# Four x tiles, chunk 0, four x tiles, chunk 2: another order of loads and engines at the start of a transformer layer

## What is computed

```python
c_act = jax.nn.silu(c)
mod = (c_act @ w_ada[l] + b_ada[l])[:, None, :]        # 1 x 6144, w_ada is 1024 x 6144
sh_m, sc_m, g_m, sh_f, sc_f, g_f = jnp.split(mod, 6, axis=-1)

u = layer_norm(x) * (1 + sc_m) + sh_m
z = u @ w_in[l]
z_pool, z_q, z_k, z_v, z_conv, z_gate = jnp.split(z, IN_SPLITS, axis=-1)
...
x = layer_norm(ALPHA * x + g_m * mix_out, ln_mix_g[l], ln_mix_b[l])
u = layer_norm(x) * (1 + sc_f) + sh_f
h = jnp.square(jax.nn.relu(u @ w_ff1[l] + b_ff1[l]))
ff_out = h @ w_ff2[l] + b_ff2[l]
```

## Time and profile before

| what | value |
|---|---|
| median of 3 runs | 1427.4 us |
| the profiled execution, its own time | 1426.88 us |
| span of the profiled execution | 1425.1 us |
| PE busy | 1393.0 us, 98% of the span |
| DVE, ACT, POOL busy | 68%, 45%, 30% |
| mean granted TensorE clock | 0.993 of full speed |

### The profile page before, as it was taken

One profiled execution on the slowest core, in us unless ns is written; L12 is line 12 of the kernel. 1 busy time (PEld: TensorE's weight loads), 2 busy tenths in 40 slices (PEclk: granted clock), 3 DMA queues, 4 the chain that ended last, 5 costly groups with the idle time before them and its releaser, 6 DMA issues.

```text
span 1425.1 us, 17299 instructions
## 1 busy us (share of the span) xinstructions
PE 1393.0 (98%) x6522; PEld 1148.6 (81%) x6522; DVE 969.4 (68%) x1340; ACT 647.3 (45%) x914; POOL 421.8 (30%) x453
## 2 busy tenths in 40 slices
PE   7799999999999999999999999999999999999996
PEld 3688888888888888888888888888888888888885
DVE  5789677776479946464768797556565646437787
ACT  5522677777542124101616774443345535343251
POOL 1006465555566000000024327333444200001315
PEclk9899999999999999999999999999999999999998
DMA  9775465654565232762622555444445878456361
GB/s 347 266 266 159 148 185 156 188 168 149 161 234 172 89 104 79 245 192 86 200 114 89 183 181 193 142 145 146 156 163 207 297 277 299 162 211 236 118 222 60
DMA packets 159083, 256.42 MB, mean 180 GB/s; under 512 B 11352, under 2 KB 81422, under 8 KB 159000
## 3 DMA queue, kind: packets, MB, share of 16 engines
q1 hardware_dynamic: 144152, 204.97, 43.1%
q0 software_dynamic: 14848, 50.34, 10.5%
HBM read 182.36 MB, written 68.71 MB: 176 GB/s over the span
## 4 chain that ended last, share of the span: by engine, by line
PE 91%; DVE 5%; ACT 2%; issue 1%; DMA 1%; SPq 0%; DVEq 0%; ACTq 0%
PE ps L2065 24%; PE ps L2067 24%; PE ps L2066 24%; PE ps L2214 11%; PE ps L2254 2%; PE ps L2264 2%; PE ps L2279 2%; PE ps L2085 1%; DVE part_lo L1922 1%; PE ps L2129 1%; PE ps L2404 1%; DVE q L1983 0%; DMA k_raw<-tw_scratch 0%; DMA ada<-in_w_ada_dram 0%; DVE w_lo L1387 0%
## 5 line engine op out<-in xcount | busy, mean ns | idle before, releaser
L2065 PE MATMUL ps<-act_hi,w_hi 128*128 128x512 f32 (+1 forms) x480 | 187.2, 390 | 9.4 <-DVE act_lo L1482 9.4
L1922 DVE TENSOR_TENSOR part_lo<-k_raw,part_hi 128x1024 fp32r<-128x1024 f32 x112 | 146.1, 1332 | 58.6 <-ACT part_hi L935 55.4
L2067 PE MATMUL ps<-act_hi,w_lo 128*128 128x512 f32 (+1 forms) x480 | 184.6, 385 | 0.0
L2066 PE MATMUL ps<-act_lo,w_hi 128*128 128x512 f32 (+1 forms) x480 | 184.6, 385 | 0.0
L2065 PE MATMUL ps<-part_hi 128*128 128x512 f32 x448 | 174.3, 389 | 0.0
L2066 PE MATMUL ps<-part_lo,part_hi 128*128 128x512 f32 x448 | 174.3, 389 | 0.0
L2067 PE MATMUL ps<-part_hi,part_lo 128*128 128x512 f32 x448 | 174.3, 389 | 0.0
L935 ACT ACTIVATE part_hi<-k_raw 128x1024 fp32r<-128x1024 f32 x112 | 116.4, 1059 | 113.6 <-DMA k_raw<-tw_scratch 48.8
L2065 PEld LDWEIGHTS ps<-act_hi,w_hi 128*128 128x128 f32 x480 | 91.1, 190 | 28.4 <-issue 5.9
L1387 DVE TENSOR_TENSOR w_lo<-w_raw,w_hi 128x1024 fp32r<-128x1024 f32 x51 | 65.9, 1291 | 65.6 <-ACT w_hi L935 65.6
L2066 PEld LDWEIGHTS ps<-act_lo,w_hi 128*128 128x128 f32 x480 | 91.2, 190 | 18.4 <-issue 1.0
(11 more groups left out here) (260 smaller groups left out, 3202.4 us busy)
## 6 DMA issues: line engine op xcount, KB each, us to landing
k_raw<-h_scratch SPq DMA_DIRECT2D x112, 256.0 KB, 4.2
w_raw<-in_w_in_dram SPq DMA_DIRECT2D x42, 512.0 KB, 4.1
ada<-in_w_ada_dram SPq DMA_DIRECT2D x8, 2048.0 KB, 9.6
tw_rows<-in_w_ff_dram POOLq DMA_DIRECT2D x64, 256.0 KB, 4.1
tw_scratch<-tw_sum POOLq DMA_DIRECT2D x32, 512.0 KB, 3.7
h_scratch<-h_sum POOLq DMA_DIRECT2D x64, 256.0 KB, 3.0
k_raw<-tw_scratch SPq DMA_DIRECT2D x64, 256.0 KB, 5.4
pair_raw<-in_w_ff_dram SPq DMA_DIRECT2D x13, 1024.0 KB, 6.3
```

Of the source, the lines that this page charges most:

```text
L1922: nc.vector.tensor_tensor(part_lo[s][:, :, :], k_raw[rs][:, :, :], f(part_hi[s][:, :, :]), ALU.subtract)\
L2065: nc.tensor.matmul(out, sh, mh, start=first, stop=False)
L2066: nc.tensor.matmul(out, sh, ml, start=False, stop=False)
L2067: return nc.tensor.matmul(out, sl, mh, start=False, stop=last)
```

## The change

The change touches the first 60 us only.

1. **Loads.** SP now issues x tiles 0 to 3, the whole of chunk 0, x tiles 4 to 7, the small rows, the whole of chunk 2, weight blocks 0 and 1, chunk 1, weight block 2, chunk 3. Before, the two halves of chunks 0 and 2 alternated with pairs of x tiles, and chunk 3 stood ahead of weight block 2. Each chunk is still two loads, for chunk 2 now 6 + 2 row blocks (`SPLIT`).
2. **PE.** Four transposed tiles, the row of chunk 0 in one piece, four transposed tiles, the row of chunk 2. PE does only k = 0..5 of chunk 2, DVE k = 6 and 7 (`ada_chunk(2)`); of chunk 3 PE does k = 0..3 (`row_chunk(3, 0)`, placed in the first projection ahead of block 2), DVE k = 4..7. `row_columns(2)` and `row_columns(3)` sum both parts, in eight matmuls instead of four. `row_columns(1)` and `(3)` move up by two k: they stand behind k = 0, 1 of block 2 instead of behind k = 3.
3. **DVE and ACT** go through the x tiles one by one, each step of a tile offset by one: statistics of tile t, then `scale_bias` of tile t-1; on ACT root of t, norm of t-1, copy of t-2. The copies of tiles 6 and 7 are now made by DVE. The copy of the bias columns (`cols`) moves behind them.
4. **`keep_active`**: 24 new transposes of the identity on PE, eight each after `row_columns(2)`, after `mod_done` 1 and after the first `u_tmp`; their output is not used.
5. Semaphore counts follow the new numbering (`N_DIRECT` 2 to 1).

The core of the diff:

```diff
-N_DIRECT = 2
+N_DIRECT = 1
+SPLIT = {0: 4, 1: 4, 2: 6, 3: 4}
...
-ADA_BANKS = {0: 0, 2: 1}
+ADA_BANKS = {0: 0, 2: 1, 3: 6}
...
-                    sp.wait_ge(partial_done, 1)
+                    sp.wait_ge(partial_done, 2)
...
+                    sp.wait_ge(partial_done, 1)
...
-                    sp.wait_ge(partial_done, 2)
+                    sp.wait_ge(head_ps_done, 5)
+                    sp.wait_ge(partial_done, 3)
...
             def load_ada_half(i, half):
-                ks = slice(4 * half, 4 * half + 4)
+                ks = (slice(0, SPLIT[i]), slice(SPLIT[i], 8))[half]
...
-            load_ada_half(0, 0)
-            load_x(range(2))
-            load_ada_half(0, 1)
-            load_x(range(2, 4))
+            load_x(range(4))
+            load_ada(0)
+            load_x(range(4, ST))
...
-            load_ada_half(2, 0)
-            load_x(range(4, 6))
-            load_ada_half(2, 1)
-            load_x(range(6, ST))
+            load_ada(2)
...
+            load_block(1)
...
-            load_block(1)
+            load_block(2)
...
-            load_block(2)
...
             def save_ada_row(i):
-                act.wait_ge(head_ps_done, {0: 1, 2: 4}[i])
+                act.wait_ge(head_ps_done, {0: 1, 2: 4, 3: 5}[i])
...
             def save_tile(i):
...
-            for i in range(0, ST, 2):
+            for i in range(ST):
...
-                take_root(i + 1, i + 1)
-                norm(i, i, mid[:, i, :])
-                if i + 1 < ST - 1:
-                    norm(i + 1, i + 1, mid[:, i + 1, :])
-                if i == 2:
-                    save_ada_row(0)
-                if i == ST - 2:
-                    save_ada_row(2)
-                    cut_hi(0)
-                    save_tile(i)
-                else:
-                    save_tile(i)
-                    save_tile(i + 1)
+                if i >= 1:
+                    norm(i - 1, i - 1, mid[:, i - 1, :])
+                if i >= 2:
+                    save_tile(i - 2)
+            save_ada_row(0)
+            save_ada_row(2)
+            cut_hi(0)
...
+            save_ada_row(3)
...
-            for i in range(0, ST, 2):
-                for t in (i, i + 1):
-                    dve.wait_ge(x_in[t], 16)
-                    stats(mid[:, t, :], t)
-                for t in (i, i + 1):
-                    scale_bias(t, t)
-                if i == 4:
-                    dve.wait_ge(head_ps_done, 3)
-                    nc.vector.tensor_copy(cols[:, 0:ROWS_A], ps[:, 7, PIECE:PIECE + ROWS_A])
-                    nc.vector.tensor_copy(cols[:, ROWS_A:ROWS_A + ROWS_C], ps[:, 7, PIECE + P:PIECE + P + ROWS_C])\
-                        .then_inc(cols_done, 1)
+            for t in range(ST):
+                dve.wait_ge(x_in[t], 16)
+                stats(mid[:, t, :], t)
+                if t >= 1:
+                    scale_bias(t - 1, t - 1)
+            scale_bias(ST - 1, ST - 1)
...
             def start_chunk(i):
...
-                dve.wait_ge(ada_in[i % 3], 16 * (i // 3 + 1))
+                if i == 1:
+                    dve.wait_ge(ada_in[1], 16)
+                elif i in (2, 3):
+                    dve.wait_ge(ada_end_in[i % 3], 16 * (i // 3 + 1))
+                else:
+                    dve.wait_ge(ada_in[i % 3], 16 * (i // 3 + 1))
...
-                link(nc.vector.tensor_scalar(partial_of(i)[:, :], ada[i % 3][:, 0, :], c_act[:, 0:1], None, ALU.mult))
-                add_rows(i, range(1, 4))
+                k0 = SPLIT[i] if i in (2, 3) else 0
+                link(nc.vector.tensor_scalar(partial_of(i)[:, :], ada[i % 3][:, k0, :], c_act[:, k0:k0 + 1], None,
+                                             ALU.mult))
+                add_rows(i, range(k0 + 1, 4))
...
             def end_chunk(i):
-                if i in (1, 3):
-                    dve.wait_ge(ada_end_in[i % 3], 16 * (i // 3 + 1))
-                add_rows(i, range(4, 8))
+                if i == 1:
+                    dve.wait_ge(ada_end_in[1], 16)
+                add_rows(i, range({2: 7, 3: 5}.get(i, 4), 8))
...
+            for t in (ST - 2, ST - 1):
+                dve.wait_ge(z_done, t + 1)
+                dve.wait_ge(x_copied, ST - 2)
+                nc.vector.tensor_copy(x_t[:, :, t * P:(t + 1) * P], tile_banks(t)).then_inc(x_copied, 1)
+            dve.wait_ge(head_ps_done, 3)
+            nc.vector.tensor_copy(cols[:, 0:ROWS_A], ps[:, 7, PIECE:PIECE + ROWS_A])
+            nc.vector.tensor_copy(cols[:, ROWS_A:ROWS_A + ROWS_C], ps[:, 7, PIECE + P:PIECE + P + ROWS_C])\
+                .then_inc(cols_done, 1)
+            ada_chunk(2)
...
-            dve.wait_ge(z_done, ST)
-            nc.vector.tensor_copy(x_t[:, :, (ST - 1) * P:ST * P], tile_banks(ST - 1)).then_inc(x_copied, 1)
...
             def row_chunk(i, half):
...
-                pe.wait_ge((ada_in, ada_end_in)[half][i % 3], 16)
-                for k in range(4 * half, 4 * half + 4):
+                pe.wait_ge((ada_in, ada_end_in)[half][i % 3], 32 if i == 3 else 16)
+                for k in range(4 if half else 0, 8 if half else SPLIT[i]):
...
-                                           start=k == 0, stop=k == 7)
+                                           start=k == 0, stop=k == (7, None, 5, 3)[i])
...
             def row_columns(i):
...
-                if i in (0, 2):
-                    pe.wait_ge(head_sb_done, 3 + i // 2)
-                else:
+                if i != 1:
+                    pe.wait_ge(head_sb_done, {0: 3, 2: 4, 3: 5}[i])
+                if i > 0:
+                    pe.wait_ge(partial_done, {2: 1, 1: 2, 3: 3}[i])
+                if i in (1, 3):
...
-                    pe.wait_ge(partial_done, 1 + i // 2)
...
-                    if i in (0, 2):
-                        ins = nc.tensor.matmul(out, ada_row[i][:, ms], ones_row[0:1, 0:1], start=True, stop=True)
-                    else:
-                        ins = nc.tensor.matmul(out, partial_of(i)[:, ms], ones_row[:, 0:1], start=True, stop=True)
+                    if i != 1:
+                        ins = nc.tensor.matmul(out, ada_row[i][:, ms], ones_row[0:1, 0:1], start=True, stop=i == 0)
+                    if i > 0:
+                        ins = nc.tensor.matmul(out, partial_of(i)[:, ms], ones_row[:, 0:1], start=i == 1, stop=True)
...
+            for i in range(4):
+                transpose_x(i)
...
-            transpose_x(0)
-            transpose_x(1)
...
-            transpose_x(2)
-            transpose_x(3)
+            for i in range(4, 7):
+                transpose_x(i)
+            transpose_x(7)
...
-            row_chunk(2, 0)
-            transpose_x(4)
+            row_chunk(2, 0).then_inc(head_ps_done, 1)
...
-            transpose_x(5)
-            row_chunk(2, 1).then_inc(head_ps_done, 1)
-            transpose_x(6)
...
-            transpose_x(7)
+
+            def keep_active():
+                for m in range(8):
+                    nc.tensor.transpose(ps[:, 0, m % 4 * P:(m % 4 + 1) * P], ident[:, :], ident[:, :])
+
+            keep_active()
+            pe.wait_ge(mod_done, 1)
+            keep_active()
+            pe.wait_ge(u_step, 1)
+            keep_active()
...
+            pe.wait_ge(mod_done, 1)
+            row_chunk(3, 0).then_inc(head_ps_done, 1)
...
-            for k in range(4):
+            for k in range(2):
...
+            for k in range(2, 4):
+                rows_part(2, k)
```

## The result

The changed kernel takes 1437.2 us (median of four runs, 1436.12 to 1439.3) against 1427.9 us (four runs, 1426.52 to 1428.69; a fourth one moved its median up from 1427.4) of the kernel before: a ratio of 1.007, 95% interval 1.0057 to 1.0083. That is 9.4 us slower; forecast were 1436.4 us, 1432.5 to 1440.0.

A forecast was written before the change was run, and what follows sets the result against it. PE was taken as the bound nearly everywhere, so a later start of its dense work moves the end; first knot +8.6 and second +0.4 gave +9.0 us, 1436.4 us, with a range of 1432.5 to 1440.0 for 8 in 10.

The forecast's parts named there:

- First knot: PE's opening of k = 0..3, up to the start of `u_tmp`: 44.4 instead of 35.77 us, costing 8.6 us.
- cold loss: Half clock in tile 3 and the row of chunk 0 after idle PE: 2.0 us taken, from 1.35 to 2.8.
- the pause ahead of tile 6: PE idles 1.5 us because ACT copies tile 4, behind chunk 0's row, before it normalises tile 6.
- Second knot: From `u_tmp` to PE's restart at k = 4: new PE work less the cold restart saved costs 0.4 us.
- `row_columns(1)` 0.9; `row_columns(3)` 1.9: Durations in us forecast for the columns of chunks 1 and 3 on PE, behind k = 0, 1 of block 2.
- Clock 1.00 there: Sign: PE idle under 1.5 us before k = 4, about 30.5 us after `u_tmp` starts, at full clock.
- Dummies without effect: The 24 `keep_active` transposes lie in pauses; the warm clock ends in a longer wait for act_lo and buys nothing.
- The fourth scale behind tile 4 as the stop: On DVE tile 3's scale waits behind tile 4's statistics, so PE transposes tile 3 only from 19.7 us.
- Nothing bites on SP: Block 2 and chunk 3 load in time; the rival, block 2 over 1.8 us later, gave 1437 to 1440, chance 0.05.
- the half clock through the whole row: Rival: chunk 0's row runs wholly at half clock, 5.0 us more, 1441 to 1443 us; chance 0.07.
- tile 4 came 0.65 us early, not by a whole place: Rival: tile 4's load overtakes part of chunk 0, at most 5.7 us earlier, giving 1430.5 to 1434; chance 0.10.
- a loss at the upper end: By the clock-gate rule scattered transposes would not warm PE, so the cold loss is at the upper end, +9.8 in all.

The follow-up runs named there:

- f1_scale3: Changed kernel, but DVE scales tile 3 right after its own statistics and ACT normalises it there, before the statistics of tile 4; 1435.4 us.
- f2_norm6: Changed kernel, but ACT normalises tile 6 before it copies tile 4; 1437.5 us.
- f4_no_dummies: Changed kernel without the 24 dummy transposes of `keep_active`; 1437.9 us.
- f3_again: Changed kernel, but DVE does all of chunk 3 and the columns of chunks 1 and 3 stand behind k = 3 of block 2; a repeat run, 1437.7 us.
- b3_row_chunk1: Kernel before, with tile 7 transposed earlier and copied by ACT, PE doing k = 0..3 of chunk 1, and columns of chunks 1 and 3 moved up; 1423.9 us.
- b1_warm: Kernel before plus 24 transposes of the identity, output unused, behind `row_columns(3)`; 1427.2 us.
- b4_columns_apart: As b3_row_chunk1, but `row_columns(1)` stands ahead of block 2, apart from `row_columns(3)`; 1424.5 us.
- f6_three: Changed kernel with three edits: tile 3 scaled before tile 4's statistics, tile 6 normalised before tile 4's copy, chunk 3 back on DVE; 1431.8 us.

## Why the prediction was right, step by step

The sum +9.0 met +9.59 at the mark and +9.4 in the medians, and the mechanism forecast is in the trace, but for the clock in the columns. Its two terms were off in opposite directions, by -0.6 and +1.1 us, so that the sum is nearer than they are; that much is luck.

**First knot, 8.6 forecast, 8.05 measured.** Step by step, forecast and measured: tile 3 from 19.7, 19.01 (tile 4 landed at 15.70, not 16.35); tile 3 and the row with the cold loss 10.06, 9.63 (cold loss 2.0 taken, 1.65 beside f1_scale3; up to 2.9 in other executions, by the 10.86 us in f2_norm6); tiles 4 and 5 with the pause ahead of tile 6 3.54, 3.43 (pause 1.5, 1.46); tiles 6 and 7 with the bias rows 2.44, 2.30; row of chunk 2 5.28, 5.24; columns of chunks 0 and 2 2.88, 3.30; from there to `u_tmp` 0.5, 0.91. The errors are -0.69, -0.43, -0.11, -0.14, -0.04, +0.42 and +0.41: together -0.58.

**Second knot, 0.4 forecast, 1.54 measured.** The mis-sized term is "`row_columns(1)` 0.9; `row_columns(3)` 1.9". The first took 0.88 (67.65 to 68.53), the second 2.60 (68.53 to 71.13). In that code a 1x1 and a 128x1 matmul alternate, each a row of x2 in the timeline, one row every 0.31 us, 2.5 us for eight of them; I had added two runs of one kind, 0.98 and 0.9. That is also the +0.42 in the columns of chunk 2. With 0.16 ahead of block 2 (U + 20.98 for U + 20.82), 0.11 in its k = 0, 1 and 0.15 behind the columns, the restart is at U + 31.6 instead of U + 30.5. From U + 28.8 that is 2.80 later; less the 1.3 us of the cold restart, which did go, 1.5.

**"Clock 1.00 there"** was true for the restart at 75.43 and not for the way to it. k = 2, 3 of block 2 ran at 0.63 us a matmul from 71.13 to 73.84. It cost nothing, because act_lo of k = 4 was ready only at 75.38 (74.15 + 1.23), just before PE took it:

```profile
74.15 1.23 DVE L1478 TENSOR_TENSOR act_lo<-u_tmp,act_hi 128x1024 fp32r<-128x1024 f32 x1 [2.40 <-ACT act_hi L934]
```

That is luck: the fall began in the columns, and there I had forecast none.

**What was right for the reason given.** Dummies without effect (f4). The fourth scale behind tile 4 as the stop (f1). Nothing bites on SP: third_hi and chunk 3 land in time, no wait for either in PE's list. Of the rivals, the half clock through the whole row did not come (8.24 us, not 14), and tile 4 came 0.65 us early, not by a whole place. The Trainium skill's "DMA: Bandwidth & Descriptors" (Queues, rings and completion order) leaves open that loads overtake; that 0.65 us is all that this trace could show of it. By the Trainium skill's "TensorE: Matmul & The Clock Gate" (Part 1: The HAM clock gate) the prediction had a loss at the upper end, 2.8 us; beside f1_scale3 it was 1.65 in the kernel after and 2.9 in f2_norm6, so some executions reach that end and others don't.

**What the forecast left out.** It counted the second knot against the kernel before. It did not ask what the same kernel would take without the row of chunk 3; f3_again (1437.7 against 1437.1 us) shows no difference.

## What to carry to other kernels

Look at an engine's order, not only at its load: the scale of one tile (two operations, 0.31 us) behind a wait for the next tile held PE for 2.6 us and cost it 1.65 us of clock besides. Fill a pause with work that was to be done anyway and can run there already, as b3_row_chunk1 does with half of chunk 1 (3.4 us together with its other steps). Dummies gave nothing that the medians show (f4_no_dummies, b1_warm), nor did half of chunk 3 in a place where PE is the bound (f3_again). Price an alternating series of tiny matmuls by a row of its own kind, not by adding rows of each kind.

## What the runs showed of the hardware

- The granted clock can fall to 0.50 while PE is busy without a gap: in the kernel after 0.5 us behind one stretch of one-column matmuls (3.3 us) and near the end of another (3.5 us), in b3_row_chunk1 2.2 us into one, in b4_columns_apart 1.3 us behind one of 2.4 us. From 70 to 1400 us of the kernel before, with 1326.5 us of busy PE and 3.7 us of such matmuls, it stays at 1.00. The cause isn't shown. The 16 of one kind in the kernel before (1.84 us) stand ahead of a pause, so nothing can be told from them.
- How long half clock lasts isn't fixed: behind the second pause 2.7 us before, 4.7 in f6_three, 4.9 in f3_again; behind a fall without a pause 3.4 us after (from 70.7), 6.8 in b3_row_chunk1. Tile 3 and the row of chunk 0 took 9.6 to 10.9 us in six executions whose pause ahead was 2.5 to 3.5 us, and 7.98 where it was 0.94. That differs by more than several of the effects studied here.
- The row of x16 takes 7.03 us at full clock and 8.24 to 9.03 behind such a pause.
- 24 transposes of the identity take 2.82 us at full clock (b1_warm) and 4.48 us where the clock has just fallen (kernel after).
